# Router on the summed rows of the output projection: norm vector moved into the router's weights, row factor moved to the logits, low halves of the rows subtracted on VectorE

## The reference

```
x = x + hybrid_mixer(h, ...)            # y @ w_out is the mixer's last step
h = rmsnorm(x, norm_ffn_g)              # x * rsqrt(mean(x*x) + EPS) * g
x = x + hierarchical_moe(h, ...)
return rmsnorm(x, final_norm_g)

# hierarchical_moe, with xt = h:
group_logits  = xt @ rg_w + rg_b        # 4 groups
expert_logits = xt @ re_w + re_b        # 32 experts
# argmax of the groups, top 2 experts in the group, gates from two softmaxes;
# tokens sorted by expert, padded blocks, silu(a) * u, down, weighted sum
```

## Time and profile before

| | |
|---|---|
| median of 3 executions | 2238.89 us |
| lowest and highest | 2238.57 and 2241.24 us |
| span of the profiled execution, first to last instruction | 2236.7 us |
| PE, DVE, ACT, POOL busy in it | 2092.9, 1404.4, 1085.2, 202.1 us |
| mean granted TensorE clock | 0.970 |

### The profile page before, as it was taken

The page is one execution under the profiler, slowest core; times in us unless marked ns, Lnnn a source line. Parts: engine busy times, 40 slices in busy tenths (PEclk is TensorE's granted clock), DMA queues, the critical chain, the costliest instruction groups (busy, mean ns, idle before and its releaser), DMA issues. The chain is left out here.

```text
span 2236.7 us, 28060 instructions
## 1 busy us (share of the span) xinstructions
PE 2092.9 (94%) x10119; PEld 1699.0 (76%) x10119; DVE 1404.4 (63%) x1815; ACT 1085.2 (49%) x1192; POOL 202.1 (9%) x207
## 2 busy tenths in 40 slices
PE   7999799999999999699999998999869999999996
PEld 5778578888888777488888887777447888888884
DVE  3543456555436555655554447887348888888887
ACT  3336614343323445514343333364327878788784
POOL 2001100000000000100000000000012222222221
PEclk9999999999999999699999999999979999999998
DMA  8232028632323221224332332310109999999995
GB/s 227 60 98 83 19 76 321 206 95 76 132 76 89 83 67 67 76 57 123 80 109 94 113 94 68 94 57 20 42 26 376 422 422 409 416 408 413 411 413 199
DMA packets 223002, 375.31 MB, mean 168 GB/s; under 512 B 12541, under 2 KB 174653, under 8 KB 200506
## 3 DMA queue, kind: packets, MB, share of 16 engines
q1 hardware_dynamic: 206282, 315.21, 40.3%
q0 software_dynamic: 12592, 44.11, 5.4%
q10 hardware_dynamic: 4032, 14.68, 1.6%
HBM read 338.27 MB, written 38.32 MB: 168 GB/s over the span
## 5 line engine op out<-in xcount | busy, mean ns | idle before, releaser
L1022 PE MATMUL PS<-XS,split 128*128 128x512 f32 (+1 forms) x2304 | 482.3, 372 | 3.6 <-DVE XS L154 3.1
L1022 PEld LDWEIGHTS PS<-XS,split 128*128 128x128 f32 x2304 | 406.7, 189 | 79.0 <-DVE XS L154 3.6
L154 DVE TENSOR_TENSOR moe_split<-moe_raw,moe_split 128x2048 fp32r<-128x2048 f32 x174 | 398.2, 2289 | 55.7 <-ACT moe_split L149 55.2
L154 DVE TENSOR_TENSOR split<-ring,split 128x2048 fp32r<-128x2048 f32 x110 | 251.6, 2290 | 270.8 <-ACT split L149 270.7
L149 ACT CAST moe_split<-moe_raw 128x2048 fp32r<-128x2048 f32 x174 | 332.8, 1913 | 11.5 <-PE PS L2661 10.8
L2639 PE MATMUL PS<-moe_split,moe_x 128*128 128x512 f32 x1392 | 336.9, 395 | 0.8 <-DVE moe_split L154 0.8
L149 ACT CAST split<-ring 128x2048 fp32r<-128x2048 f32 x110 | 209.5, 1905 | 200.2 <-PE PS L1058 110.8
L2639 PEld LDWEIGHTS PS<-moe_split,moe_x 128*128 128x128 f32 x1392 | 257.3, 188 | 52.8 <-DVE moe_split L154 1.2
L2661 PE MATMUL PS<-moe_split,moe_h 128*128 128x512 f32 x696 | 164.8, 393 | 1.7 <-DVE moe_h L154 1.4
L2661 PEld LDWEIGHTS PS<-moe_split,moe_h 128*128 128x128 f32 x696 | 128.5, 188 | 33.2 <-DVE moe_h L154 7.1
L1058 PE MATMUL PS<-split,XS 128*128 128x512 f32 x672 | 152.6, 390 | 0.0
(11 more groups left out here) (389 smaller groups left out, 2634.6 us busy)
## 6 DMA issues: line engine op xcount, KB each, us to landing
moe_raw<-in_expert_w_gate SPq DMA_DIRECT2D x58, 1024.0 KB, 7.0
moe_raw<-in_expert_w_up SPq DMA_DIRECT2D x58, 1024.0 KB
moe_raw<-in_expert_w_down SPq DMA_DIRECT2D x58, 1024.0 KB, 7.1
ring<-in_w_up SPq DMA_DIRECT2D x88, 512.0 KB, 5.1
ring<-in_w_down SPq DMA_DIRECT2D x44, 512.0 KB, 4.1
expert_rows<-rows POOLq DMA_DIRECT2D x4, 4096.0 KB, 30.9
expert_rows<-W ACTq DMA_DIRECT2D x28, 512.0 KB
ring<-in_w_in SPq DMA_DIRECT2D x24, 512.0 KB, 5.3
```

The source lines that it names most:

```text
L154: return dve.tensor_tensor(lo, raw, hi.bitcast(F32), ALU.subtract)
L1022: mm = pe.matmul(PS[:, b + q, rows], w[:, c, q, :], x_half(k, high)[:, c, rows], start=(c == 0 and m == 0), stop=(c == KC - 1 and m == 2))
```

## The change

Four things are done.

1. `turn` transposes the summed rows X[t] after `summed`, no longer the normed rows after `normed`. The norm vector is loaded as eight more columns of `chan` (one more small DMA and 8 more columns of one transpose early in the program; `chan` grows by 32 bytes in each partition, and so all tiles allocated behind it begin 32 bytes later). DVE multiplies it into the router's table `rw` once (`between`, for t = 2), and PE's first `logits` waits for that with `table_scaled`. The row factor 1/rms is multiplied to the logits by four DVE instructions, which also add the bias.
2. The PSUM banks with the transposed rows are copied to XT by DVE (`leave_turned`) and no longer by ACT. The copy stands in DVE's stream behind `varied` and ahead of the reciprocal and the norm of the same tile.
3. ACT makes `row_high` of tile t right behind that tile's norm. DVE subtracts `row_low` of tile t - 1 ahead of its sum of tile t, and that of the last tile behind the first one-hot matrices. POOL subtracts nothing any more.
4. DVE computes the small tables of the routing ahead of its wait for the logits.

```
-    src = (lambda t: X[:, t, :]) if mode == "ln" else (lambda t: hrow[:, t % nh, :])
+    src = (lambda t: hrow[:, t % nh, :]) if mode == "ln+rms" else (lambda t: X[:, t, :])
+    turnable = summed if mode == "rms" else normed
...
     def turn(pe, t):
-        pe.wait_ge(normed, t + 1)
+        pe.wait_ge(turnable, t + 1)
...
+            if not split:
+                tail.rows_high(act, t)
+                continue
             for half in range(2):
                 act.wait_ge(turned, 2 * t + half + 1)
...
+    def leave_turned(dve, t):
+        for half in range(2):
+            dve.wait_ge(turned, 2 * t + half + 1)
+            dve.tensor_copy(k.XT[:, 4 * half:4 * half + 4, t * P:(t + 1) * P],
+                            PS[:, turn_pair[t] + half, :].rearrange("p (c n) -> p c n", c=4)).then_inc(xt_out, 1)
+
     def vector(dve):
         dve.wait_ge(rows_in, 16 * len(gains))
         for t in range(NT):
             if t == NT - 1 and tail.early:
                 tail.early.vector(dve)
+            if not split:
+                tail.between(dve, t)
             dve.wait_ge(product, t + 1)
...
                 dve.drain().then_inc(varied, 1)
-                if split and t > 0:
+                if not split:
+                    leave_turned(dve, t)
+                elif t > 0:
                     low(dve, t - 1)
...
-                              (64, 1, A["mlstm_norm_g_2"][0].rearrange("(n p) -> n p", p=P))]:
+                              (64, 1, A["mlstm_norm_g_2"][0].rearrange("(n p) -> n p", p=P)),
+                              (68, 1, A["norm_ffn_g_2"][0].rearrange("(n p) -> n p", p=P))]:
...
         if t == 0:
-            pe.wait_ge(s.table_in, 80)
+            pe.wait_ge(s.table_scaled, 1)
...
+    def rows_high(act, t):
+        act.wait_ge(normed, t + 1)
+        act.copy(row_high[:, t, :], h[:, t, :]).then_inc(s.row_halves, 1)
+
+    def rows_low(dve, t):
+        dve.wait_ge(s.row_halves, t + 1)
+        split_low(dve, h[:, t, :], row_high[:, t, :], row_low[t]).then_inc(s.row_lows, 1)
+
+    def between(dve, t):
+
+        if t == 2:
+            dve.wait_ge(s.table_in, 80)
+            dve.tensor_tensor(rw, rw, along(gain_col, 36), ALU.mult).then_inc(s.table_scaled, 1)
+        if t > 0:
+            rows_low(dve, t - 1)
...
-        dve.wait_ge(s.table_in, 80)
-        dve.wait_ge(s.logits, NT)
-        dve.tensor_tensor(L, PS[:, 6, 0:144].rearrange("p (t n) -> p t n", t=NT), across(rb, NT), ALU.add)
         dve.tensor_copy(tok_i, tokf)
...
+        dve.wait_ge(s.logits, NT)
+        for t in range(NT):
+            dve.scalar_tensor_tensor(L[:, t, :], PS[:, 6, 36 * t:36 * t + 36], st[:, t, 15:16], rb, ALU.mult, ALU.add)
+        dve.drain()
...
         block_places(dve, 0, slot_iota)
-
+        rows_low(dve, NT - 1)
...
-        for t in range(NT):
-            pool.wait_ge(s.row_halves, t + 1)
-            split_low(pool, h[:, t, :], row_high[:, t, :], row_low[t]).then_inc(s.row_lows, 1)
...
+                if t == NT - 1:
+                    pe.wait_ge(s.row_lows, NT)
...
-            pe.wait_ge(s.row_lows, NT)
+            pe.wait_ge(s.row_lows, NT - 1)
```

More of the change, by code:

```diff
@@ L859, in scalar @@
                 tail.early.scalar(act)
+            if not split:
+                tail.rows_high(act, t)
+                continue
             for half in range(2):
                 act.wait_ge(turned, 2 * t + half + 1)
-                to = x_half(k, 1) if split else k.XT
-                act.copy(to[:, 4 * half:4 * half + 4, t * P:(t + 1) * P],
+                act.copy(x_half(k, 1)[:, 4 * half:4 * half + 4, t * P:(t + 1) * P],
                          PS[:, turn_pair[t] + half, :].rearrange("p (c n) -> p c n", c=4))\
-                   .then_inc(xt_high if split else xt_out, 1)
+                   .then_inc(xt_high, 1)
     def low(dve, t):
@@ L905, in vector @@
                 g = k.rows[:, 2 if mode == "ln+rms" else 0, :]
-                if t >= nh:
+                if split and t >= nh:
                     dve.wait_ge(turned, 2 * (t - nh + 1))
@@ L1635, in gpsimd @@
                               (60, 1, A["conv_ln_b_2"][0].rearrange("(n p) -> n p", p=P)),
-                              (64, 1, A["mlstm_norm_g_2"][0].rearrange("(n p) -> n p", p=P))]:
+                              (64, 1, A["mlstm_norm_g_2"][0].rearrange("(n p) -> n p", p=P)),
+                              (68, 1, A["norm_ffn_g_2"][0].rearrange("(n p) -> n p", p=P))]:
             pool.dma_start(rows[at:at + src.shape[0], half, :], src).then_inc(rows_in, 16)
     def tensor(pe):
-        pe.wait_ge(rows_in, 128)
+        pe.wait_ge(rows_in, 144)
         pe.transpose(PS[:, 6, 0:128], rows[:, 0, :], k.ident)
-        pe.transpose(PS[:, 6, 128:196], rows[0:68, 1, :], k.ident[0:68, 0:68]).then_inc(turned, 1)
+        pe.transpose(PS[:, 6, 128:204], rows[0:76, 1, :], k.ident[0:76, 0:76]).then_inc(turned, 1)
     def scalar(act):
         act.wait_ge(turned, 1)
-        act.copy(k.chan[:], PS[:, 6, 0:196]).then_inc(k.cols_in, 1)
+        act.copy(k.chan[:], PS[:, 6, 0:204]).then_inc(k.cols_in, 1)
     return dict(gpsimd=gpsimd, tensor=tensor, scalar=scalar)
@@ L2264, in moe_stages @@
     rb = room(36)
+    gain_col = k.chan[:, 196:204]
     iota = room(64 + P)
@@ L2301, in moe_stages @@
              "x_in x_turned xh_out xl_out w_high used silued mids mid_turned mh_out ml_out y_kept y_saved "
-             "found0 found1 found2 found3 combined rooted final out_saved0 out_saved1 out_saved2 out_saved3 "
+             "found0 found1 found2 found3 combined rooted final table_scaled out_saved0 out_saved1 out_saved2 out_saved3 "
              "gain_in all_saved counted first_placed last_slots late_ready end_kept end_put row_halves row_lows x_rows x_kept x_kept2 paired summed sums_turned").split()
@@ L2365, in route_tensor @@
         pe.transpose(PS[0:32, 7, 256:384], block_expert, k.ident).then_inc(s.sums_turned, 1)
+    def rows_high(act, t):
[10 more added lines that the diff above has]
+            rows_low(dve, t - 1)
+    k.tail.rows_high, k.tail.between = rows_high, between
     def route_scalar(act):
-        act.wait_ge(product_1, NT)
-        for t in range(NT):
-            act.wait_ge(normed, t + 1)
-            act.copy(row_high[:, t, :], h[:, t, :]).then_inc(s.row_halves, 1)
         act.wait_ge(s.gexp, 1)
@@ L2988, in program @@
             k.small[:, i * P:(i + 1) * P] for i in range(4))
-        k.chan = sb("chan", [P, 196])
+        k.chan = sb("chan", [P, 204])
         k.lam = sb("lam", [P, 8])
```

4 lines of the change are left out of this document (1 added, 3 removed).

## The result

The changed kernel is slower: 2248.49 us median (2246.66 to 2249.61, 5 runs) against 2238.57 us, ratio 1.0042 with a 95% interval of 1.0032 to 1.0053. Timed once more, beside other runs of before, it gave 2247.14 us and 1.0027 (1.0015 to 1.0039). So 6 to 10 us are lost, where I had expected 2 and called it unmeasurable. The profiled span is 2246.8 us.

A forecast was written before the change was run, and what follows sets the result against it. Bound taken: PE until the last router product, then DVE's routing up to its first maximum. Terms +2.9 + 2.5 - 6.2 + 2.6 = +1.8 us gave 2240.7 us, range 2235.7 to 2244.3, no measurable change expected.

The forecast's parts named there:

- part 4: Last low half on DVE delays POOL's scatter and block 2's gather; 1.3 us claimed covered, costing nothing.
- Term 5: PE's clock falls at the wait ahead of the first logits, before product 3: +2.6 us, bounds 0 and 3.5.
- Rival A: Clock stays up at the wait ahead of the first logits: -0.8 us in sum, 2238.1 us; chance 18%.
- B: Product 3 mostly at the lower clock, deciding from some 10.5 us: +4.5 to +15, about 2246 us; chance 10%.
- Terms 1, 2 and 3: First logits wait for DVE, +2.9 us; last sum later, +2.5; tables ahead of logits, no POOL beside them, -6.2.
- Rival C: Terms 1 and 2 largely absent, for instance through unseen PE slack; only the 6.2 us gain left: 2232.7 us; chance 5%.
- Rival D: Tiles behind `chan` begin 32 bytes later, slowing transfers: expert loop a per cent, 5 us, longer; chance 2%.
- the 0.45 us: Time from the turn's start until its first half is turned, used in the first-logits wait of +2.9 us.

The follow-up runs named there:

- Experiment 8: Kernel before plus four idle DVE copies ahead of the slot numbers: 2245.14 us, ratio 1.0016; with nine copies: 2244.68 us, 1.0021.
- experiment 6: All low halves on POOL: changed kernel with scaling early 2234.41 us (0.9970); that with the column's own load 2236.20 (0.9978); changed kernel, scaling late, 2241.49 (1.0002).
- Experiment 2: Changed kernel with DVE scaling the router's table ahead of its copy of tile 1: 2240.89 us, ratio 1.0010.
- experiments 4: Changed kernel, table scaled early, DVE summing each tile before finishing the one before: 2236.19 us (0.9983); also with last low half behind slot numbers: 2234.34 (0.9976).
- experiment 5: Kernel before with only the small tables ahead of the wait for the logits, POOL's subtractions left: 2239.34 us, ratio 1.0000.
- experiments 1: Kernel before plus only the norm vector's column in `chan`: 2240.64 us (1.0008); changed kernel with the column loaded on its own, `chan` as before: 2245.94 (1.0024).

## Why the prediction was wrong

**What failed is part 4, "What is hidden": "so 1.3 us are covered".** I followed the delayed scatter only to the issue of the gather and argued that blocks 0 and 1 come from `hot`. I never read when the gather lands and when PE needs it. The trace of before has it (`--source L2582`, window 1700 to 1710), for the gather issued at 1704.32:

```profile
DMA to landing us min/median/max: 9.8/9.8/9.8
```

So it landed at 1714.1, for a turn at 1716.56: a cover of 2.5 us. That alone would have hidden 1.3 us. But I took a delay of the scatter by 1.3 us for a delay of the gather by 1.3 us. The scatter that starts later runs into DVE's three subtractions of weights (6.78 us without a gap) and into the second batch of weight loads, and stretches from 24.5 to 28.6 us. So the gather was issued 5.2 us later against the first one-hot product (1.1 from the low half, 4.1 from the stretching), not 1.3. It landed 8.5 us behind its issue this time, 1.2 quicker, and PE came to its turn 1.0 us sooner: 5.2 - 1.2 + 1.0 - 2.5 of cover are 2.5 us, and the wait is 2.58. Over all kernels of the table the wait follows the time from scatter to gather: none at 23.8 to 24.5 us, 0.1 to 0.2 at 26.4 to 27.1, 2.5 to 3.7 at 28.5 or more. Experiment 8 shows it with no other edit, and in experiment 6 it goes with the low halves. In the local stretch it costs 3.2 us: 2.6 of wait, 1.6 of cold product, less 1.0.

With these 3.2 us my sum would have been +5.0 and the time 2243.9 us, still within my range. That the first comparison lies beyond it, at 2248.49, is also due to 4 us that the change does not explain (below).

What stretches the scatter has two parts. That single issues of POOL take up to 2.9 us beside DVE's 2048-column subtractions and 1.0 elsewhere stands in the rows: each issue that was held ended 0.8 us behind the end of the subtraction that was running when it began (1699.37 + 1.99 = 1701.36 in the changed kernel, against about 1700.5 for the end of the second of the three that start at 1695.94). The Trainium skill, DMA: Bandwidth & Descriptors, section "SWDGE vs HWDGE vs iDMA", says that GpSimd writes the descriptors of its DMAs to SBUF, and that DVE can lock it out there; these rows agree, with 2.87 us for 0.97. The Trainium skill speaks there of a mode of DVE; whether these subtractions run in it, no run here shows. That the wait for the last landing is 5.1 to 6.0 us instead of 2.9 to 3.7 because weight loads are on the queues is only argued: it is late where the last scatter's issue ends past SP's next pair of loads (1701.36 against 1698.91 in the changed kernel), and early where it ends ahead of it (1691.41 against 1693.81 before, and 1686.70 against 1689.07, landing 3.31, with scaling early and the low halves on POOL), but I did not move those loads. In all kernels the landing is also late just where the last issue itself was held by DVE (1.90 to 2.23 us), and early where it took 0.97, so these runs can't tell the two causes apart.

**Term 5, the clock, was right in kind and too small**: 1.3 in the logits and 2.1 in product 3, 3.4 us for my 2.6, within my bounds. The windows of PE:

```profile
1636.00:1637.00 1.00, 0.44 (x5) 0.47 (x5) 0.41 (x2) 0.93 (x1) 0.00 (x0) 1.00 0.15 57
1637.00:1638.00 1.00, 1.00 (x7) 1.00 (x7) 0.85 (x1) 0.12 (x1) 0.00 (x0) 0.52 1.00 401
1643.00:1644.00 1.00, 1.00 (x3) 0.43 (x2) 0.00 (x0) 0.00 (x0) 0.00 (x0) 0.57 0.00 0
1645.00:1646.00 1.00, 1.00 (x3) 0.38 (x2) 0.00 (x0) 0.00 (x0) 0.00 (x0) 1.00 0.00 0
```

(The last four numbers of a row are POOL's share, the granted clock, the DMA share and GB/s.) The clock was still granted in full in the microsecond in which the first logits began (1636.56), and was lower from the next one until past 1643: some 7 us, where I had taken 5 to 6 from the two returns in the earlier trace rows. Rival A (the clock stays up) did not occur; B's 10.5 us were not reached.

**Terms 1, 2 and 3 held**: +2.84 for 2.9, +2.2 for 2.5, -6.0 for -6.2. Experiment 2 removes the first, experiments 4 and 6 the second. Rival C, slack that hides both, is out by the same rows. For the third, the fast tables of experiment 5 beside a new slow instruction show that the gain is due to POOL's absence at that moment. The Trainium skill, SBUF — State Buffer, section "SBUF: two separate sides", would have it so, and the trace agrees: 1.40 us for an instruction that takes 0.18 without POOL. Experiment 6 shows in addition that POOL need not be idle, only elsewhere: with scaling early the first reduction comes 0.9 us behind the last logits and no maximum is slow. With scaling late one maximum took 1.61 us for 0.17, so it matters where POOL's last subtraction falls.

**Rival D, slower transfers**, is not borne out: 1.0008 for the column alone, and the opposite sign in experiment 6. From the turn of block 3 to the end of the span go 502.3 us before, 502.9 in the changed kernel, and 502.5 to 503.2 in the kernels of experiments 1 and 6, with the wider `chan` or without.

**Slips in the sums.** The lower end of my range takes off 2.4 us "for the best of the terms", but the bounds of terms 1, 2 and 3 give 1.3. In rival D one beat of 32 bytes more in a packet of 2 KB is 1 in 64, 1.6% and not 1.4%. PE reads the last low half as the eighth operand, after seven products, not six. And the 0.45 us are counted from product 3's end, 0.6 from the start of the turn. None of them decides anything.

**What is left of the first result.** Local terms give +5.8 of the span's +10.1. The rest of the span (span less local stretch) was 2102.9 us in the profile of before and 2107.1 in that of the changed kernel; in all other kernels it lay between 2101.3 and 2107.7, and the three with the code of before up to this place had 2105.4, 2106.0 and 2107.7. So the profile of before was among the quick ones there, and the later timings of before had medians up to 2241.06 us. Windows show one of the places (granted clock 1.00 and 0.57), before and then after:

```profile
138.00:142.00 4.00, 3.48 (x13) 1.62 (x13) 2.29 (x1) 4.00 (x7) 0.00 (x0) 1.00 0.01 3
```

```profile
138.00:142.00 4.00, 4.00 (x11) 1.40 (x10) 2.29 (x1) 4.00 (x7) 0.00 (x0) 0.57 0.00 0
```

The kernel with only the tables moved, whose code is that of before there, was at 0.70 in this window, that with four idle copies at 1.00, and that with only the column at 1.00. So the column does not cause it; what decides it from one execution to the next stays open. The repeat's 6.1 us fits the local 5.8, the first 9.9 does not, and I can't say more than that 4 us of the first comparison are not explained by the change.

## What to carry to other kernels

A step that is delayed off the critical path must be followed to the instruction that finally needs its result, through the queues and with the landing time of the transfer, and the slack read there: here it was 2.5 us, and a delay of 1.2 grew to 5.2 on its way to the gather's issue. Work taken from a slow engine is no gain where that engine had idle time under long products; with scaling early, moving it in time (each low half behind its tile) kept the gain without the waits. A small operand that the dense engine waits for belongs ahead of anything that waits for that engine.

## What the runs showed of the hardware

- A scatter issue on POOL took 0.96 to 1.07 us alone and 1.9 to 2.9 us when it began beside one of DVE's 2048-column subtractions (1.77 beside the 1024-column low half). In one of the profiles an issue that began just behind such a subtraction, at 1683.41 for 1683.39, was not held (0.97 us).
- A DVE instruction on 16 elements took 1.4 to 2.4 us beside POOL's subtractions and 0.17 without them.
- A wait of 2.84 us and narrow logits cost another 3.4 us by the clock; a wait of 2.58 us between dense products cost 1.6 (7.34 for 5.74), while one of 0.2 cost nothing (5.75). A wait of 2.6 us ahead of product 1 cost 1.7 in four of the profiles (15.70 for 14.00) and nothing in the others.
- An indirect gather of 128 rows landed 8.5 to 11.1 us behind its issue in the expert loop.
